# Output projection of two layers in high and low parts, with the expert weights on another order of slots

## The reference

```python
def hybrid_mixer(h, w_in, q_norm_g, w_q_up, kv_norm_g, w_uk, w_uv, w_o, pos, slopes, n_keep):
    proj = h @ w_in
    qa, kva, kr, dq, dk, dv, iq, ik, iw = jnp.split(proj, SPLIT_POINTS, axis=-1)
    out_a = mla_group(qa, kva, kr, q_norm_g, w_q_up, kv_norm_g, w_uk, w_uv, pos)
    out_b = dsa_group(dq, dk, dv, iq, ik, iw, slopes, n_keep)
    return jnp.concatenate([out_a, out_b], axis=-1) @ w_o

for l in range(DEPTH):                      # DEPTH = 2
    mix = hybrid_mixer(x, ...)
    x = layer_norm(ALPHA * x + mix, ln1_g[l], ln1_b[l])
    ffn = grouped_moe(x, router_w, router_bias, w_gate[l], w_up[l], w_down[l])
    x = layer_norm(ALPHA * x + ffn, ln2_g[l], ln2_b[l])
```

## Time and profile before

| | before |
|---|---|
| median of 3 runs | 1495.42 us |
| profiled execution, own time | 1495.48 us |
| its span, first to last instruction | 1493.4 us |
| PE busy | 1357.7 us (91%), 7728 matmuls |
| PEld (weight loads of TensorE) busy | 953.5 us (64%) |
| DVE busy | 706.3 us (47%) |
| ACT busy | 506.2 us (34%) |
| POOL busy | 120.7 us (8%) |
| chain that ended last | PE 80%, DVE 7%, DMA 5%, ACT 3% |
| granted TensorE clock, mean | 0.958 of full |

### The profile page before, as it was taken

One profiled execution on the slowest core, in us unless ns is written; L12 is line 12 of the kernel. 1 busy time (PEld: TensorE's weight loads), 2 busy tenths in 40 slices (PEclk: granted clock), 3 DMA queues, 4 the chain that ended last, 5 costly groups with the idle time before them and its releaser, 6 DMA issues.

```text
span 1493.4 us, 19713 instructions
## 1 busy us (share of the span) xinstructions
PE 1357.7 (91%) x7728; PEld 953.5 (64%) x7728; DVE 706.3 (47%) x1355; ACT 506.2 (34%) x929; POOL 120.7 (8%) x135
## 2 busy tenths in 40 slices
PE   6998799999699897999987899789999888899997
PEld 3864534443367544443436888479998685599985
DVE  0644411121416532121216589577785636377766
ACT  1342312111122621121114422236664445167553
POOL 1011000000000300000002064030000003000000
PEclk9999799999899998999997999899999998999999
DMA  9444299999926129999997525846665440455750
GB/s 322 181 150 170 113 388 420 421 420 421 371 105 226 57 103 373 421 421 422 419 406 244 168 85 116 163 153 208 194 240 198 144 141 1 141 169 169 244 179 28
DMA packets 128048, 347.71 MB, mean 233 GB/s; under 512 B 8208, under 2 KB 84262, under 8 KB 103396
## 3 DMA queue, kind: packets, MB, share of 16 engines
q1 hardware_dynamic: 122576, 330.19, 58.9%
q0 software_dynamic: 4528, 15.84, 4.5%
q10 hardware_dynamic: 868, 0.63, 0.2%
HBM read 342.44 MB, written 4.19 MB: 232 GB/s over the span
## 4 chain that ended last, share of the span: by engine, by line
PE 80%; DVE 7%; DMA 5%; ACT 3%; SPq 2%; issue 2%; POOL 0%; DVEq 0%; ACTq 0%
PE bank L1559 17%; PE bank L1756 12%; PE bank L1895 8%; PE bank L1896 7%; PE bank L1897 7%; PE bank L1766 6%; DMA slot<-in_w_up 4%; PE bank L1777 2%; PE bank L2016 2%; PE bank L2020 2%; PE bank L2018 2%; SPq L622 2%; PE bank L1930 2%; ACT arena L813 1%; DVE res L1106 1%
## 5 line engine op out<-in xcount | busy, mean ns | idle before, releaser
L1895 PE MATMUL bank<-x_high,w_high 128*128 128x256 f32 x912 | 261.6, 287 | 0.0
L1896 PE MATMUL bank<-x_low,w_high 128*128 128x256 f32 x912 | 260.6, 286 | 0.0
L1897 PE MATMUL bank<-x_high,w_low 128*128 128x256 f32 x912 | 260.5, 286 | 0.0
L1756 PE MATMUL bank<-slot,arena 128*64 128x512 f32 x1024 | 224.2, 593 | 12.1 <-DMA slot<-in_w_up 5.6
L758 ACT ACTIVATE w_high<-slot 128x1024 fp32r<-128x1024 f32 x174 | 174.2, 1051 | 171.8 <-PE bank L1897 91.1
L1895 PEld LDWEIGHTS bank<-x_high,w_high 128*128 128x128 f32 x912 | 177.9, 195 | 1.8 <-issue 1.6
L1896 PEld LDWEIGHTS bank<-x_low,w_high 128*128 128x128 f32 x912 | 177.8, 195 | 0.0
L1897 PEld LDWEIGHTS bank<-x_high,w_low 128*128 128x128 f32 x912 | 177.7, 195 | 0.0
L1756 PEld LDWEIGHTS bank<-slot,arena 128*64 128x64 f32 x1024 | 76.0, 137 | 156.9 <-issue 156.9
L758 ACT ACTIVATE arena<-bank 128x512 f32<-128x512 f32 (+6 forms) x136 | 69.4, 520 | 245.5 <-PE bank L1813 86.9
L1559 PE MATMUL bank<-slot,arena 128*128 128x512 f32 (+1 forms) x320 | 141.0, 601 | 4.4 <-ACT arena L758 3.5
(11 more groups left out here) (276 smaller groups left out, 1910.1 us busy)
## 6 DMA issues: line engine op xcount, KB each, us to landing
slot<-in_w_gate SPq DMA_DIRECT2D x64, 1024.0 KB, 19.7
slot<-in_w_up SPq DMA_DIRECT2D x64, 1024.0 KB, 18.0
slot<-in_w_down SPq DMA_DIRECT2D x64, 1024.0 KB, 21.5
slot<-in_ffn_w_in SPq DMA_DIRECT2D x44, 1024.0 KB, 7.5
slot<-in_ffn_w_out SPq DMA_DIRECT2D x22, 1024.0 KB, 5.0
slot<-in_hgrn_w_in SPq DMA_DIRECT2D x16, 1024.0 KB, 7.0
slot<-in_w_in SPq DMA_DIRECT2D x10, 1024.0 KB, 11.4
slot<-in_w_o SPq DMA_DIRECT2D x8, 1024.0 KB, 7.1
```

The lines of the kernel that those rows point to most:

```text
L1756: last = mm(banks_gu["gu".index(m)][rows, :], xe[:, 4 * half + c, rows], ws[e][:, c, :], start=(half == 0 and c == 0), stop=(half == 1 and ...
L1895: mm(dst, high[:, k, :], x_high[:, k, :], start=(k == 0), stop=False)
L1896: mm(dst, high[:, k, :], x_low[:, k, :], start=False, stop=False)
L1897: last = mm(dst, low[:, k, :], x_high[:, k, :], start=False, stop=(k == KD - 1))
```

## The change

1. The output projection of layers 0 and 1 is `split_out`: three fp32r products for each fp32 product. ScalarE writes O of pair j straight into `x_high` and VectorE the rest into `x_low` (`low_mix`), which now drains the bank. w_o is cut into eight halves; the two `w_high` and two `w_low` buffers hold four halves in a ring. Halves 0 to 3 are cut between the q copies, 4 to 7 after the attention loop, each when TensorE has used the one before it in its place (`out_used`).
2. TensorE takes block j (chunk j of the width) for all four banks for j = 0 to 3, then tile 0's four blocks, then tile 1's.
3. In `softmax_heads`, ScalarE copies O of pair p-4 ahead of the exponentials of pair p. Layer 3 uses the same function.
4. The mixer's weights turn through slots 0 to 5. The experts' loads go in blocks of six to slots 0 to 5, 12 to 17, 6 to 11 in turn, and the last block of a layer to 12 to 17. In each layer the first load to a slot of 6 to 11 waits for y11.
5. Banks of the norm are fixed: y00 to y11 in 0 to 3, the transposes in 4 to 7, the router's in 0 and 1. The counts of `split` in later layers move up by the new halves.

```diff
+OUT_UNIT = [0, 4]
+HG_UNIT = 8
...
-            load((l, f"wo{n}"), (l, "y11"))
+            load((l, f"wo{n}"), ("split", 2 * (OUT_UNIT[l] + n + 1), 0))
...
+        blocks = [(None, NSLOT, RAW_SLOTS)[n % 3] for n in range(12 * PAIRS // RAW_SLOTS - 1)] + [NSLOT]
+        places = [b if b is None else b + i for b in blocks for i in range(RAW_SLOTS)]
...
-                if u.place >= NSLOT and (name[0], u.place) not in begun:
-                    produced(sp, (name[0], f"O{HEADS - 1}"))
+                if u.place >= RAW_SLOTS and (name[0], u.place) not in begun:
+                    produced(sp, (name[0], f"O{HEADS - 1}" if u.place >= NSLOT else "y11"))
...
+            def split_out(l, j):                      # ScalarE
+                if j % 2 == 0:
+                    loaded(act, (l, f"wo{j // 2}"))
+                if j >= 4:
+                    act.wait_ge(sem("out_used"), 4 * l + j - 3)
+                copy(ring_half(w_high, j), out_half(l, j)).then_inc(sem("high_ready"), 1)
...
             def softmax_heads(l, heads, probs, probsT, outT, sink=False):
                 for p in range(heads // 2 + 4):
+                    if 0 <= p - 4:
+                        b = produced(act, (l, f"O{p - 4}"))
+                        if l < DEPTH:
+                            copy(outT[:, p - 4, :], b[:, 0:T]).then_inc(sem("mix_high"), 1)
+                        else:
+                            drained(copy(outT[:, p - 4, :], b[:, 0:T]), (l, f"O{p - 4}"))
                     for k in (2 * p, 2 * p + 1) if p < heads // 2 else ():
...
-                    if 0 <= p - 4:
-                        b = produced(act, (l, f"O{p - 4}"))
-                        drained(copy(outT[:, p - 4, :], b[:, 0:T]), (l, f"O{p - 4}"))
...
-                softmax_heads(l, 2 * HEADS, A["prob"], A["probT"], A["mixT"])
+                softmax_heads(l, 2 * HEADS, A["prob"], A["probT"], x_high)
+                for j in range(4, 8):
+                    split_out(l, j)
...
+            def low_out(l, j):                        # VectorE
+                dve.wait_ge(sem("high_ready"), 2 * OUT_UNIT[l] + j + 1)
+                V.tensor_tensor(ring_half(w_low, j), out_half(l, j), ring_half(w_high, j).bitcast(F32), ALU.subtract).then_inc(sem("split"), 1)
+
+            def low_mix(l, j):
+                b = produced(dve, (l, f"O{j}"))
+                dve.wait_ge(sem("mix_high"), HEADS * l + j + 1)
+                drained(V.tensor_tensor(x_low[:, j, :], b[:, 0:T], x_high[:, j, :].bitcast(F32), ALU.subtract), (l, f"O{j}"))
...
                 dve.wait_ge(sem("kr_roped"), l + 1)
+                for j in range(4):
+                    low_out(l, j)
...
+                    if p >= 4:
+                        low_mix(l, p - 4)
                     if 1 <= p <= HEADS:
                         reciprocals(l, p - 1)
...
+            def split_out(l):                         # TensorE
+                bs = [[reuse(pe, (l, f"y{t}{h}")) for h in range(2)] for t in range(NT)]
+                def block(j, t, h):
+                    c, dst = slice(512 * h, 512 * (h + 1)), bs[t][h][:, :]
+                    high, low = (ring_half(w, j)[:, c] for w in (w_high, w_low))
+                    mm(dst, x_high[:, j, tok(t)], high, start=(j == 0), stop=False)
+                    mm(dst, x_high[:, j, tok(t)], low, start=False, stop=False)
+                    last = mm(dst, x_low[:, j, tok(t)], high, start=False, stop=(j == KD - 1))
...
+                def ready(j):
+                    evacuated(pe, (l, f"O{j}"))
+                    pe.wait_ge(sem("split"), 2 * OUT_UNIT[l] + j + 1)
+                for j in range(4):
+                    ready(j)
+                    for t in range(NT):
+                        for h in range(2):
+                            last = block(j, t, h)
+                    last.then_inc(sem("out_used"), 1)
+                for j, h in ((4, 0), (5, 0), (6, 0), (4, 1), (5, 1), (7, 0), (6, 1), (7, 1)):
+                    if h == 0:
+                        ready(j)
+                    block(j, 0, h)
+                for h in range(2):
+                    for j in range(4, 8):
+                        block(j, 1, h)
...
-                for j in range(HEADS):
-                    evacuated(pe, (l, f"O{j}"))
-                project_out(l, "y", A["mixT"], ["wo0", "wo1", "wo2", "wo3"])
+                split_out(l)
```

## The result

| | before | after |
|---|---|---|
| median, us | 1494.91 (4 runs, 1493.93 to 1495.9) | 1473.84 (4 runs, 1473.69 to 1475.77) |
| ratio after to before | | 0.9854, 95% interval 0.9842 to 0.9866 |
| span of the profiled execution, us | 1493.4 | 1472.1 |
| PE, DVE, ACT busy, us | 1357.7, 706.3, 506.2 | 1340.2, 730.3, 522.2 |

The change makes the kernel faster by 21.1 us in the medians and 21.3 in the profiled spans. The changed kernel was timed once more beside the last experiments: 1475.4 us, ratio 0.9872 (0.9853 to 0.9891), span 1473.8; that lies inside the range, so the median alone doesn't say how far the forecast was off, and the spans and their parts do.

A forecast was written before the change was run, and what follows sets the result against it. TensorE's rate was taken to bound the output projection, with everything up to the experts hanging on it. (8.7 - 0.75) + (8.6 - 0.75) - 2 x 0.5 + 1.0 = 15.8 us won, so 1479.7 us; range 1474 to 1488.

The forecast's parts named there:

- A: Rival: TensorE's clock falls at the projection as before, 3.4 us less won, 1483.1 us; chance 0.22.
- D: Rival: the projection's products don't hide their weight loads, 0.39 us each, slower at 1509 us; chance 0.05.
- The projection: Output projection, layers 0 and 1: 96 products at 0.226 us, 21.9 us with drain; 8.7 and 8.6 us won.
- The clock behind O7: Projection's start, layers 0 and 1: full clock holds (6 in 10) with the gap filled; else 1.7 us lost per layer.
- The loop: Attention loops: VectorE's added subtractions against gaps and removed waits, 0.5 us lost per layer in 0 and 1.
- What the order gives back: Norm behind the projection, layers 0 and 1: VectorE reaches y11 later after the new block order, 0.75 us lost per layer.
- The weight stream: Loads ahead of the experts: thirteen loads end at 172.7, landing by 177, all 18 slots full in time; cost 0.
- E: The time y11 is full in the projection; y00 was to be full at E-6.8, VectorE at y11 at E+0.8.
- C: Rival: slots are empty when the experts begin and the stream swallows the gain, 1494 to 1497 us; chance 0.07.
- Ring and early splits: Halves 4 to 7 ready in time (slack 1.0 us), splits among q copies covered by 2.0 to 4.3 us; cost 0.

The follow-up runs named there:

- the slots without the parts: Kernel before with the six-slot plan and ScalarE's O copies ahead of the exponentials, projection kept in fp32: 1511.15 us, ratio 1.0102.

## Why the forecast was right in kind and too small

The direction and most of the mechanism held, and rivals A and D did not come. The sum fell short by 5.5 us of 21.3 in the spans: 1.7 in the attention loops of layers 0 and 1, 1.7 in the clock of layer 3's projection, 0.7 in VectorE's lateness and 1.5 spread over the rest. The step that failed is the one on the attention loop, which took VectorE's subtraction to lengthen the loop; beside it the sum has no term for TensorE's clock in layer 3, without a reason given.

- *The projection.* 0.226 us for each of 96 products and 21.9 us in all: measured 0.227 and 22.0., a stretch of the same three parts elsewhere in the kernel, was the right row, and D had no ground.
- *The clock behind O7.* It held, as taken. The run with a wait for O7 shows what it would have cost: 1.6 us a layer beside the gap, near the 1.7 named. In nine profiles the projection follows O7 at once behind a loop at the full clock, and it took 22.0 us in both layers each time. But the reason given, that the level holds through gaps of 0.88 us and falls after one of 1.25, does not stand. The kernel before has the half clock behind gaps of 1.10 us in layers 1 and 3, and the changed kernel has the full one behind 1.10 in layer 3; with the reordered copies alone there is both in one trace, full behind 1.10 in layer 0, half behind 1.18 in layer 1; and with the slots without the parts it is full behind 1.25. The length of the gap does not settle it, and what does stays open: the forecast of the clock was right here, its reason was not.
- *The clock in layer 3.* It was not in the sum. In the nine profiles with the reordered copies in front of that fp32 projection (the changed kernel's two, and seven experiments) it took 27.7 us, in the two without them 29.4. So the 1.7 us go with the reorder; by which part of it is not shown. In layers 0 and 1 three of the four fp32 projections behind reordered copies took 27.7 us as well (two runs), and neither of the two without.
- *The loop.* This is the step that failed. Forecast: 0.5 us lost in each of layers 0 and 1, from 4 x 0.42 = 1.7 of VectorE's work against short gaps and two waits of TensorE, of 0.7 together. Measured: 0.38 and 0.36 won. The two waits were right: the reorder brings 0.62. The price of the work was wrong: the subtraction does take 0.42 on VectorE, but costs the loop 0.25 in all, not the 1.2 that lie between 0.7 won and 0.5 lost. In layer 0 the O products start 2.56 us apart with the reordered copies alone; with the subtractions two of the seven distances are 2.68 and the others still 2.56. So VectorE did not bound this loop. 1.7 us of the shortfall.
- *What the order gives back.* 0.75 forecast, 0.42 measured. The prediction's own terms, 1.44 + 4.64 + 1.44 = 7.52 from E-6.8, give E+0.72, which it put at E+0.8; and they were read from rows that each stood behind a wait. Without a wait VectorE goes from y00's start to y11 in 7.23 us. 0.67 us in two layers.
- *The weight stream.* Cost 0, as forecast: the experts took 207.9 and 208.5 us before, 207.8 and 208.3 after, and the stream stood still ahead of them. The stream was to end at 172.7 and ended near 174.3 (139 GB/s from 173 to 174, 25 in the next us, then none); the next transfer starts near 179, when the experts have begun to free slots. The runs show how thin this is: loads that start at y11 cost 9 to 12 us a layer, so some 20 in all, where the forecast's rival gave the whole gain, 16. C was no idle fear, and had 0.07 for a sound reason: the release by the split.
- *Ring and early splits.* TensorE waited for no half, and the q products kept their place (77.47 against 77.94; the 0.5 us come from the clock in the first projections). VectorE's rotation began 1.5 us later, 88.02 for 86.50, and TensorE still had the rotated q when it asked, at 96.11 for 96.58. Cost 0 and 0, as taken.
- *The rest.* 1.5 us are the sum of differences of both signs where the kernels do not differ, mostly in the clock: 0.5 won in the first projections, 1.2 won between y11 and the experts in layer 0, 0.8 lost there in layer 1, and smaller ones between layers. The same kernel's second profile is 1.7 us longer, so this line is within what chance does to one trace. A range that ended at 1474.0 left no room for that on the low side, though it did for 8 us on the other.

## What to carry to other kernels

When one engine's new instruction reads what another engine writes, the order on the writing engine changes its price: the reordered copies alone brought some 4 us in the kernel before, and once VectorE depended on them, taking them back cost 23.7. A ring that gets smaller is paid for by when its places come back, so look at the first held place in the loading queue, and not at the length of the stage. And before work is moved onto VectorE with both inputs in SBUF, look at what GpSimd does at that time; if it is long, cut it, put gaps between the pieces and start it behind that work; cutting alone left VectorE's wait as long as it was.

## What the hardware showed that was not expected

- GpSimd's addition of 13.14 us held a 1.21 us subtraction of VectorE for 14.6 us. Cut into 16 instructions of nearly 1 us back to back, it held three subtractions for 16.64 us in all (3.48 when undisturbed): VectorE got no turn between them. In pairs with some 9.4 us between them, and begun 20 us later, they cost little: the pair at 986.05 lengthened a small VectorE instruction to 0.99 us and two subtractions from 2.36 to 2.86.
- In the kernel before and after, the same addition lengthens a VectorE instruction on 128x8 elements, with one SBUF tensor as input, to 11 us (970.21 to 981.18 in the changed kernel). TensorE did not wait for it, so it cost TensorE nothing, and no wait of TensorE showed it, only the row of VectorE itself.

```profile
967.74 13.40 POOL L746 TENSOR_TENSOR arena<-arena 128x6144 f32<-128x6144 f32 x1
970.21 10.97 DVE L1522 TENSOR_SCALAR arena<-arena 128x8 f32 x1 [1.50 <-ACT arena L766]
```

- The same idle gap of TensorE was followed by the full clock in some stages and half of it in others: 1.10, 1.18 and 1.25 us each have both.
